# A fused two-block network: the SSM chunk-end products, their evictions and the scan, one projection tile later

## The chip, the cores and the metric

One core of a Trainium2 chip runs the whole program in one launch. The metric is device time in microseconds (us), as the median of several executions; lower is better. TensorE (PE, with PEld for its weight loads), VectorE (DVE), ScalarE (ACT), GpSimd (POOL) and SyncE (SP, which issues the weight loads) each run their own instruction stream in order and meet at semaphores.

## The reference, cut to what matters

The reference is two blocks one behind the other on 512 tokens of width 1024. The first is an attention and MLP network. The second is a hybrid layer: one projection gives queries, keys and values of 12 attention heads, the input `u` of a state space model (SSM) and two gates. The change sits in the second block, in the part that works on `u`:

```python
z = n @ w_in                       # 4 tiles of u, 12 heads x (q, k, v), gates
uf = u.astype(jnp.float32).reshape(B, S, SSM_GROUPS, SSM_GROUP)
bu_re = jnp.einsum('bsgc,gpc->bsgp', uf, bb_re)
bu_im = jnp.einsum('bsgc,gpc->bsgp', uf, bb_im)
_, _, h_re, h_im = lax.associative_scan(_complex_affine_combine, (ar, ai, bu_re, bu_im), axis=1)
y = (jnp.einsum('bsgp,gcp->bsgc', h_re, c_re.astype(jnp.float32))
     - jnp.einsum('bsgp,gcp->bsgc', h_im, c_im.astype(jnp.float32))
     + d_skip.astype(jnp.float32) * uf)
```

## The kernel before, in words

Every projection runs through one pipeline. A unit is a weight tile of 8x128x128 floats. SyncE loads it into `raw` (4 slots), ScalarE rounds it to `w_hi` (L1731, 2 slots), GpSimd computes the remainder `w_lo = raw - w_hi` (L919), and TensorE does 24 products of 128x512 for it (L1097, L1098, L1099, three for each of 8 slices). ScalarE makes the `w_hi` of tile t+1 when it comes to tile t, after tile t-1 has been finished on TensorE, and then does its own duties for tile t-1.

The second block's projection is one long list of tiles, `middle`: 4 tiles of `u`, then for each head n the tiles (n, 0) query, (n, 1) key and (n, 2) value, then the gates. The work of attention and of the SSM is hung on these tiles by hand, in each engine's `middle_after` or `middle_tile`. Behind tile (n, x) there come:

- TensorE, x = 0: the products of probabilities and values of head n-2 (L1556, L1555), the turning of the values of head n-1 (L1157) and its scores (`group_scores`, L1529). The scores wait for the semaphore `roped` of head n-1 and for `s_stored`. x = 2: the turning of the probabilities of head n-1 (L1157).
- VectorE, every tile: the eviction of the accumulator (L3211 and L3213, for values L3213 alone), after which the accumulator is free (`stored`). x = 0: masks and row maxima of head n-1 (`group_tops`, L3243, L3249). x = 2: `add_rotated` (L3224), which ends in `roped`, and at the end of the tile the eviction L3257 of the outputs of head n-1 (`group_outputs`).
- ScalarE, x = 0: the exponentials of head n-1. They wait for the negated maxima (L3249), and ScalarE's next `w_hi` stands behind them. x = 1: the two DMAs of `rotate`, which wait for the key tile's eviction. x = 2: copies of the turned probabilities.

The SSM works on chunks of 8 tokens. Its input goes out to DRAM and comes back by chunk as `u_chunk`: ScalarE issues four of the eight DMAs at tile (0, 0) and four at (0, 1). `chunk_ends` on TensorE (L1469) is 128 products of 64x64 into four PSUM banks, `keep_ends` on VectorE copies these banks to `state` (L3274), and `scan` on VectorE is a generator of 78 instructions: 35 large ones (L3141 to L3149, seven rounds of five, 128x256 or 128x128), 35 small ones (the same lines at 128x32 and 128x16) and 8 of 128x784 (L3166 to L3172, twice four). A table in VectorE's `middle_tile` says how many of them are issued behind each tile of heads 1 to 4. They come before `group_outputs` of an x = 2 tile, and behind the eviction of every tile. The end of the scan is waited for by TensorE at `ssm_outputs`, behind tile (5, 1).

The order on each engine is therefore the order of the code; no scheduler is in it. The lines that follow are those of the profile.

Of the kernel before, what the change touches and what calls it, by code (L numbers as in the profile page):

```python
# [207 lines left out]
def transposed_blocks_program(nc, a, out):  # L208
# [84 lines left out]
    with ctx:  # L293
# [383 lines left out]
        for i in range(8):  # L677
            for t in range(4):
# [3 lines left out]
                n = (hi - lo) * P  # L682
# [44 lines left out]
        def others(T, kind=""):  # L727

            b = take(T, kind)
            T.saw(f"{kind}full{b}")  # L730
            T.saw(f"{kind}stored{b}")
            return b
# [222 lines left out]
        def _(pe):  # L955
            T = start(pe)
# [619 lines left out]
            def middle_after(t):  # L1576
                kind, n, x = MID[t]
                if kind == "qkv":
                    if x == 0 and n:
                        if n > 1:  # L1580
                            group_values(n - 2)
                        turn_values(n - 1)
                        group_scores(n - 1)
                    if x == 2 and n:
                        turn_probs(n - 1)
                    if (n, x) == (1, 0):
                        chunk_ends()
                    if n == 5 and x:
                        ssm_outputs(x - 1)
                    if n in (9, 10) and x == 1:  # L1590
                        turn_outputs(n - 9)
                if kind == "gate_ssm":
                    if n == 0:
                        group_values(LAST_STEP - 1)
                        turn_values(LAST_STEP)
                        group_scores(LAST_STEP)
                    if n == 1:
                        group_values(LAST_STEP)
                        turn_rows()
                if (kind, n) in SPREAD_AT:  # L1600
                    spread_weights(SPREAD_AT[kind, n])
                if kind == "glu_b":
                    if n == 0:
                        turn_probs(LAST_STEP)
                if (kind, n) == ("gate_attn", 1):
                    T.saw("attended")
                    pe.wait_ge(sems["attended"], T.at("attended"))
# [97 lines left out]
        def _(act):  # L1705
            T = start(act)
# [578 lines left out]
            def middle_tile(m, s, t, b):  # L2285
                kind, n, x = MID[t]
                if kind == "u":
                    send_u(n, b)
                    if n == 3:
                        turn_angles()  # L2290
                if kind == "qkv":
                    if n == x == 0:
                        fetch_u(0, 4)
                    if x == 0:
                        if n > 1:
                            others(T, "o_")
                        if n:
                            copy_values(n - 1)
                            group_exponentials(n - 1)
                        if n == 1:  # L2300
                            for _ in range(2):
                                others(T, "t_")
                                others(T, "o_")
                    if x == 1:
                        rotate(n)
                        if n == 0:
                            fetch_u(4, CHUNK)
                    if x == 2:
                        T.saw("roped")
                        if n:  # L2310
                            copy_probs(n - 1)
                    if (n, x) == (2, 0):
                        fetch_toe()
                    if (n, x) == (3, 1):
                        fetch_ca()
                    if n == 5 and x:
                        keep_outputs(x - 1)
                    if n == 6 and x:
                        square_outputs(x - 1)
                    if n in (7, 8) and x == 2:  # L2320
                        gelu_gate(n - 7)
                    if n in (9, 10) and x == 1:
                        round_y(n - 9)
                G = gtmp[:, n % 2]
                if (kind, n) == ("gate_attn", 0):
                    round_attention(3)
                if kind in ("gate_ssm", "gate_attn"):
                    stored(b)
                    fn(G[:, 0, :], G[:, 0, :], ACT.Sigmoid).then_inc(sems["gate"], T.up("gate"))
                if kind == "gate_ssm":  # L2330
                    if n == 0:
                        others(T, "o_")
                        copy_values(LAST_STEP)
                        group_exponentials(LAST_STEP)
                    if n == 1:
                        others(T, "o_")
                    if n == 1:
                        for _ in range(2):
                            others(T, "t_")
                    if n == 4:  # L2340
                        round_shares()
                for _ in SPREAD_AT.get((kind, n), ()):
                    others(T, "o_")
                if kind == "glu_a":
                    if n in (6, 7):
                        round_attention(n - 5)
                if kind == "glu_b":
                    act.wait_ge(sems[f"full{b}"], T.at(f"full{b}"))
                    if n >= 2:
                        act.wait_ge(sems["gated"], T.at("gated", 1))  # L2350
                    fn(G[:, 1, :], acc2[b], ACT.Sigmoid).then_inc(sems[f"stored{b}"], T.up(f"stored{b}"))
                    T.saw("gated")
                    if n == 2:
                        weigh()
                    if n == 5:
                        round_attention(0)
                    if n == 0:
                        copy_probs(LAST_STEP)
                if kind == "attn":
                    T.saw("gated")  # L2360
                    act.wait_ge(sems["gated"], T.at("gated"))
                    fn(mixed_hi[:, n, :], G[:, 0, :], ACT.Copy).then_inc(sems["mixed_hi"], T.up("mixed_hi"))
# [90 lines left out]
        def _(dve):  # L2453
# [813 lines left out]
            def keep_ends():  # L3267

                v.memset(state[:, :, :, 0:1], 0.0).then_inc(sems["dve"], T.up("dve"))
                for ri, kind in ((0, "t_"), (1, "o_")):  # L3270
                    for f in range(2):
                        b = result(T, kind)
                        dve.wait_ge(sems[f"{kind}full{b}"], T.at(f"{kind}full{b}"))
                        v.tensor_copy(state[:, ri, 8 * f:8 * f + 8, 1:],  # L3274
                                      (tps, ops_)[ri][b].rearrange("p (j k) -> p j k", j=8)).then_inc(
                            sems[f"{kind}stored{b}"], T.up(f"{kind}stored{b}"))
                for kind in ("t_stored0", "t_stored1", "o_stored0", "o_stored1"):
                    dve.wait_ge(sems[kind], T.at(kind))
# [115 lines left out]
            def middle_tile(m, s, t, b):  # L3394
# [9 lines left out]
                if kind == "qkv":  # L3404
                    if (n, x) == (0, 0):
                        make_tables()
                    group_tile(n, x, b)
                    if x == 2:
                        add_rotated(n)
                    if x == 0 and n:  # L3410
                        others(T, "t_")
                        group_tops(n - 1)
                        if n == 1:
                            keep_ends()
                    if x == 2 and n:
                        probs_turned(n - 1)
                    if (n, x) == (0, 1):
                        invert_root_h()
                    if 1 <= n <= 4 and (n, x) != (1, 0):
                        for _ in range(((0, 8, 8), (4, 7, 7), (9, 10, 10), (7, 4, 4))[n - 1][x]):  # L3420
                            next(scanning, None)
                    if n == 5:
                        if x == 0:
                            assert not list(scanning)
                        else:
                            for _ in range(2):
                                others(T, "o_")
                    if n and x == 2:
                        group_outputs(n - 1)
                    if n in (7, 8) and x == 1:  # L3430
                        cube(n - 7)
                    if n in (8, 9) and x == 2:
                        gate_y(n - 8)
                    if n in (9, 10) and x == 1:
                        rest_of_y(n - 9)
# [179 lines left out]
```

## Time and profile before

| what | value |
|---|---|
| median of 3 runs | 2124.36 us (2124.08 to 2124.7) |
| the profiled execution's own time | 2126.04 us |
| its span | 2124.2 us |
| TensorE busy | 2109.9 us (99%) |
| TensorE weight loads busy | 1804.1 us (85%) |
| VectorE busy | 1127.6 us (53%) |
| GpSimd busy | 873.1 us (41%) |
| ScalarE busy | 818.2 us (39%) |
| granted TensorE clock, mean | 0.998 of full |

The shares are means over the whole span. The stretch in question, tile (1, 0) to tile (5, 1), runs from about 1237 to 1340 us. In a timeline each row has start, duration, engine, line, operation, out<-in, how many; what stands in brackets is the idle time before it and what ended it. An instruction that is queued behind a running one or blocked in its access shows as a long duration and not as idle time.

### The profile page before, as it was taken

What the parts mean: (1) busy time and instruction counts of PE and PEld (TensorE: products, weight loads), DVE (VectorE), ACT (ScalarE), POOL (GpSimd) and SP (SyncE); (2) the same over time, 40 slices, a digit from 0 to 9 for tenths busy, and PEclk for the clock granted to TensorE, in tenths of its full rate; (3) what the DMA queues carried; (4) which work ended last, traced back from release to release, by engine and by line L of the source; (5) the groups of instructions that cost most, each with busy time, mean ns of one, the idle gap of its engine ahead of it and who ended that gap; (6) DMA issues with size and microseconds to landing.
All of it is one profiled execution on the core that took longest, in us unless ns stands there. A gap on an engine that the chain in (4) does not pass through costs nothing.

```text
span 2124.2 us, 33781 instructions
## 1 busy us (share of the span) xinstructions
PE 2109.9 (99%) x13386; PEld 1804.1 (85%) x13386; DVE 1127.6 (53%) x1701; ACT 818.2 (39%) x1362; POOL 873.1 (41%) x379
## 2 busy tenths in 40 slices
PE   9999999999999999999999999999999999999998
PEld 9987899999999777888888788888887788888887
DVE  6678766525632476420333579566774644543125
ACT  5258544223323584421333323344433432322224
POOL 3313434434444554444444433243444444444442
PEclk9999999999999999999999999999999999999999
DMA  6610245343434403333333465233233233333331
GB/s 178 168 56 2 56 140 144 90 120 103 137 90 134 133 2 92 97 95 94 92 96 94 134 130 153 79 86 86 86 88 95 87 112 89 99 89 92 89 101 66
DMA packets 375411, 210.77 MB, mean 99 GB/s; under 512 B 26659, under 2 KB 367876, under 8 KB 374392
## 3 DMA queue, kind: packets, MB, share of 16 engines
q1 hardware_dynamic: 364974, 192.61, 31.8%
q10 hardware_dynamic: 10314, 16.41, 2.8%
q8 instruction: 90, 1.47, 0.3%
q14 instruction: 33, 0.27, 0.0%
HBM read 196.97 MB, written 15.40 MB: 100 GB/s over the span
## 4 chain that ended last, share of the span: by engine, by line
PE 59%; issue 27%; POOL 12%; DVE 0%; ACT 0%; DMA 0%; POOLq 0%; SPq 0%; DVEq 0%; ACTq 0%
PE acc L1097 15%; PE acc L1098 15%; PE acc L1099 15%; POOL w_lo L919 12%; PE acc L1185 3%; PE ops L1254 2%; PE tps L1194 1%; PE acc L979 1%; PE ops L1248 1%; PE acc L980 1%; PE acc L981 1%; PE tps L1157 1%; DMA xin<-in_x 0%; PE ops L1409 0%; SPq L740 0%
## 5 line engine op out<-in xcount | busy, mean ns | idle before, releaser
L919 POOL TENSOR_TENSOR w_lo<-raw,w_hi 128x1024 fp32r<-128x1024 f32 x326 | 800.1, 2454 | 1126.5 <-ACT w_hi L1731 1116.0
L1731 ACT ACTIVATE w_hi<-raw 128x1024 fp32r<-128x1024 f32 x325 | 344.5, 1060 | 1005.5 <-PE acc L1099 985.7
L1097 PE MATMUL acc<-hr_hi,w_hi 128*128 128x512 f32 x1056 | 421.4, 399 | 0.1
L1099 PE MATMUL acc<-hr_hi,w_lo 128*128 128x512 f32 x1056 | 417.7, 396 | 0.0
L1098 PE MATMUL acc<-hr_lo,w_hi 128*128 128x512 f32 x1056 | 417.6, 395 | 0.0
L1097 PE MATMUL acc<-hn_hi,w_hi 128*128 128x264 f32 (+1 forms) x840 | 246.7, 294 | 0.0
L1099 PE MATMUL acc<-hn_hi,w_lo 128*128 128x264 f32 (+1 forms) x840 | 244.2, 291 | 0.0
L1098 PE MATMUL acc<-hn_lo,w_hi 128*128 128x264 f32 (+1 forms) x840 | 244.2, 291 | 0.0
L1097 PEld LDWEIGHTS acc<-hr_hi,w_hi 128*128 128x128 f32 x1056 | 198.5, 188 | 48.6 <-issue 1.1
L1099 PEld LDWEIGHTS acc<-hr_hi,w_lo 128*128 128x128 f32 x1056 | 198.4, 188 | 47.9
L1098 PEld LDWEIGHTS acc<-hr_lo,w_hi 128*128 128x128 f32 x1056 | 198.5, 188 | 47.3 <-issue 0.7
L1098 PEld LDWEIGHTS acc<-hn_lo,w_hi 128*128 128x128 f32 x840 | 158.3, 188 | 2.7
L1097 PEld LDWEIGHTS acc<-hn_hi,w_hi 128*128 128x128 f32 x840 | 158.2, 188 | 2.8
L1099 PEld LDWEIGHTS acc<-hn_hi,w_lo 128*128 128x128 f32 x840 | 157.5, 188 | 2.5
L1097 PE MATMUL acc<-mid_hi,w_hi 128*128 128x264 f32 x512 | 145.5, 284 | 0.0
L1098 PE MATMUL acc<-mid_lo,w_hi 128*128 128x264 f32 x512 | 145.0, 283 | 0.0
L1099 PE MATMUL acc<-mid_hi,w_lo 128*128 128x264 f32 x512 | 145.0, 283 | 0.0
L942 POOL TENSOR_SCALAR probs<-probs,stat 128x528 f32<-128x528 f32 (+2 forms) x49 | 72.8, 1486 | 104.5 <-DVE stat L2581 104.5
L1097 PE MATMUL acc<-mr_hi,w_hi 128*128 128x512 f32 x256 | 101.2, 396 | 0.0
L1098 PE MATMUL acc<-mr_lo,w_hi 128*128 128x512 f32 x256 | 101.2, 396 | 0.0
L1099 PE MATMUL acc<-mr_hi,w_lo 128*128 128x512 f32 x256 | 101.2, 396 | 0.0
L1097 PEld LDWEIGHTS acc<-mid_hi,w_hi 128*128 128x128 f32 x512 | 96.4, 188 | 0.2 <-issue 0.2
(486 smaller groups left out, 3755.6 us busy)
## 6 DMA issues: line engine op xcount, KB each, us to landing
raw<-in_w_up SPq DMA_DIRECT2D x64, 512.0 KB, 4.0
raw<-in_w_down SPq DMA_DIRECT2D x64, 512.0 KB, 3.9
raw<-in_w_in SPq DMA_DIRECT2D x56, 512.0 KB, 3.8
raw<-in_w_ffn_gate SPq DMA_DIRECT2D x22, 512.0 KB, 3.7
raw<-in_w_ffn_up SPq DMA_DIRECT2D x22, 512.0 KB, 3.8
raw<-in_w_in_even SPq DMA_DIRECT2D x18, 512.0 KB, 7.1
raw<-in_w_ffn_down SPq DMA_DIRECT2D x16, 512.0 KB, 3.8
raw<-in_w_in_odd SPq DMA_DIRECT2D x10, 512.0 KB, 5.4
```

The source lines that it names most:

```text
L919: nc.gpsimd.tensor_tensor(w_lo[:, part], raw[:, slot], w_hi[:, part].bitcast(F32), ALU.subtract).then_inc(sems["lo"], T.up("lo"))
L942: nc.gpsimd.tensor_scalar(S, S, st[:, 4:5], None, ALU.mult).then_inc(sems["scaled"], T.up("scaled"))
L979: mm(out, w_hi[:, part, k, :], x_hi, start=first, stop=False)
L980: mm(out, w_hi[:, part, k, :], x_lo, start=False, stop=False)
L981: return mm(out, w_lo[:, part, k, :], x_hi, start=False, stop=last)
L1097: mm(out, w_hi[:, part, w0 + k, :], xh, start=s0, stop=False)
L1098: mm(out, w_hi[:, part, w0 + k, :], xl, start=False, stop=False)
L1099: ins = mm(out, w_lo[:, part, w0 + k, :], xh, start=False, stop=s1)
L1157: ins = nc.tensor.transpose(out(t), x, ident[k:k + x.shape[0], k:k + x.shape[0]])
L1185: ins = mm(bank[rows, c:c + w], q, keys, start=first, stop=last)
L1254: ins = mm(ops_[b][rows, to], p.v[o][k], weights(o, k)[:, queries], start=k == 0, stop=k == last)
L1731: fn(w_hi[:, n % 2], raw[:, n % 4], ACT.Copy).then_inc(sems["hi"], T.up("hi"))
```

## The change

The chunk-end products, their evictions and the bookkeeping of their banks on ScalarE move from tile (1, 0) to tile (1, 1). The scan starts behind tile (1, 2) instead of (1, 1). Its table goes from 0, 8, 8 / 4, 7, 7 / 9, 10, 10 / 7, 4, 4 for the tiles of heads 1, 2, 3, 4 to 0, 0, 9 / 6, 9, 9 / 9, 10, 10 / 9, 7, 4. The new numbers sum to 82, so the generator runs out at tile (4, 1), one tile earlier than before.

```diff
@@ TensorE, middle_after
-                    if (n, x) == (1, 0):
+                    if (n, x) == (1, 1):
                         chunk_ends()
@@ ScalarE, middle_tile
-                        if n == 1:
-                            for _ in range(2):
-                                others(T, "t_")
-                                others(T, "o_")
+                    if (n, x) == (1, 1):
+                        for _ in range(2):
+                            others(T, "t_")
+                            others(T, "o_")
@@ VectorE, middle_tile
-                        if n == 1:
-                            keep_ends()
+                    if (n, x) == (1, 1):
+                        keep_ends()
...
-                    if 1 <= n <= 4 and (n, x) != (1, 0):
-                        for _ in range(((0, 8, 8), (4, 7, 7), (9, 10, 10), (7, 4, 4))[n - 1][x]):
+                    if 1 <= n <= 4 and (n, x) > (1, 1):
+                        for _ in range(((0, 0, 9), (6, 9, 9), (9, 10, 10), (9, 7, 4))[n - 1][x]):
                             next(scanning, None)
```

On TensorE, behind tile (1, 0), the order before is as follows. L1157 and L1529 are the turned values and the scores of head 0, L1469 the chunk ends, L1097 to L1099 a projection tile.

```order
L1157 MATMUL tps<-ident,qkv 128x128 x4
L1529 MATMUL acc<-qkv 128x128
L1529 MATMUL acc<-qkv 128x256 x3
L1469 MATMUL tps<-u_chunk,ends_w 64x64 x32
L1469 MATMUL ops<-u_chunk,ends_w 64x64 x32
L1097 MATMUL acc<-hr_hi,w_hi 128x512
```

In the changed kernel the same products stand behind tile (1, 1), whose last products are the first rows here.

```order
L1098 MATMUL acc<-hr_lo,w_hi 128x512
L1099 MATMUL acc<-hr_hi,w_lo 128x512
L1469 MATMUL tps<-u_chunk,ends_w 64x64 x32
L1469 MATMUL ops<-u_chunk,ends_w 64x64 x32
L1097 MATMUL acc<-hr_hi,w_hi 128x512
```

So a whole tile of 24 products now lies between the scores of head 0 and the chunk ends. On VectorE, in the key tile (2, 1) and up to the rotation L3224 in the value tile (2, 2), there stands before:

```order
L3213 TENSOR_TENSOR qkv<-acc,rope_c 128x512
L3141 TENSOR_TENSOR scan_tmp<-state,a_pow 128x256
L3143 TENSOR_TENSOR scan_tmp<-state,a_pow 128x256
L3145 TENSOR_TENSOR state<-state,scan_tmp 128x32x8
L3147 TENSOR_TENSOR state<-state,scan_tmp 128x16x8
L3149 TENSOR_TENSOR state<-state,scan_tmp 128x16x8
L3141 TENSOR_TENSOR scan_tmp<-state,a_pow 128x256
L3143 TENSOR_TENSOR scan_tmp<-state,a_pow 128x256
L3213 TENSOR_TENSOR qkv<-acc,rstd 128x512
L3224 TENSOR_TENSOR qkv<-qkv,rot_s 32x1024
```

and in the changed kernel:

```order
L3213 TENSOR_TENSOR qkv<-acc,rope_c 128x512
L3141 TENSOR_TENSOR scan_tmp<-state,a_pow 128x256
L3143 TENSOR_TENSOR scan_tmp<-state,a_pow 128x256
L3145 TENSOR_TENSOR state<-state,scan_tmp 128x32x8
L3147 TENSOR_TENSOR state<-state,scan_tmp 128x16x8
L3149 TENSOR_TENSOR state<-state,scan_tmp 128x16x8
L3141 TENSOR_TENSOR scan_tmp<-state,a_pow 128x256
L3143 TENSOR_TENSOR scan_tmp<-state,a_pow 128x256
L3145 TENSOR_TENSOR state<-state,scan_tmp 128x32x8
L3147 TENSOR_TENSOR state<-state,scan_tmp 128x16x8
L3213 TENSOR_TENSOR qkv<-acc,rstd 128x512
L3224 TENSOR_TENSOR qkv<-qkv,rot_s 32x1024
```

Two scan instructions more stand ahead of the rotation of head 2 in this tile. On VectorE again, from the key tile (4, 1) to the rotation of head 4, before:

```order
L3213 TENSOR_TENSOR qkv<-acc,rope_c 128x128x4
L3166 TENSOR_TENSOR scan_tmp<-state,a_pow 128x784
L3168 TENSOR_TENSOR scan_tmp<-state,a_pow 128x784
L3170 TENSOR_TENSOR state<-state,scan_tmp 128x16x7x7
L3172 TENSOR_TENSOR state<-state,scan_tmp 128x16x7x7
L3213 TENSOR_TENSOR qkv<-acc,rstd 128x128x4
L3224 TENSOR_TENSOR qkv<-qkv,rot_s 32x1024
```

and in the changed kernel:

```order
L3213 TENSOR_TENSOR qkv<-acc,rope_c 128x128x4
L3168 TENSOR_TENSOR scan_tmp<-state,a_pow 128x784
L3170 TENSOR_TENSOR state<-state,scan_tmp 128x16x7x7
L3172 TENSOR_TENSOR state<-state,scan_tmp 128x16x7x7
L3166 TENSOR_TENSOR scan_tmp<-state,a_pow 128x784
L3168 TENSOR_TENSOR scan_tmp<-state,a_pow 128x784
L3170 TENSOR_TENSOR state<-state,scan_tmp 128x16x7x7
L3172 TENSOR_TENSOR state<-state,scan_tmp 128x16x7x7
L3213 TENSOR_TENSOR qkv<-acc,rstd 128x128x4
L3224 TENSOR_TENSOR qkv<-qkv,rot_s 32x1024
```

All four instructions that stood behind the rotation of head 4 are now ahead of it, and one of the eight has moved to tile (4, 0).

## Rows read from the trace of the kernel before

**Rows 1.** The page: the span, and busy time by engine.

```profile
span 2124.2 us, 33781 instructions
PE 2109.9 (99%) x13386; PEld 1804.1 (85%) x13386; DVE 1127.6 (53%) x1701; ACT 818.2 (39%) x1362; POOL 873.1 (41%) x379
```

**Rows 2.** TensorE's waits over the whole span: us in total, times, longest.

```profile
PE tps L1469 <- DMA u_chunk<-u_d: 1.6, 1, 1.6
...
PE acc L1097 <- POOL w_lo L919: 0.2, 1, 0.2
```

**Rows 3.** Timeline of TensorE behind tile (1, 0): start, us, instruction.

```profile
1242.93 1.68 PE L1529 MATMUL acc<-qkv 128*128 128x128 f32 x8
1246.26 2.08 PE L1469 MATMUL tps<-u_chunk,ends_w 128*64 128x64 f32 x64 [1.65 <-DMA u_chunk<-u_d]
...
1250.14 0.50 PE L1097 MATMUL acc<-hr_hi,w_hi 128*128 128x512 f32 x1
```

**Rows 4.** Timeline of TensorE behind tile (2, 0).

```profile
1269.79 1.68 PE L1529 MATMUL acc<-qkv 128*128 128x128 f32 x8
1271.12 0.58 PE L1097 MATMUL acc<-hr_hi,w_hi 128*128 128x512 f32 x1
```

**Rows 5.** Timeline of TensorE: behind (1, 2); head 2's scores; tile (3, 2); head 4's scores.

```profile
1261.44 0.93 PE L1157 MATMUL tps<-ident,probs 128*128 128x128 f32 x7
...
1290.86 1.68 PE L1529 MATMUL acc<-qkv 128*128 128x128 f32 x8
...
1297.97 0.40 PE L1097 MATMUL acc<-hr_hi,w_hi 128*128 128x512 f32 x1
...
1333.07 1.06 PE L1529 MATMUL acc<-qkv 128*128 128x128 f32 x8
```

**Rows 6.** Timeline of VectorE: a round of the scan and tile (3, 0)'s eviction.

```profile
1292.88 0.44 DVE L3149 TENSOR_TENSOR state<-state,scan_tmp 128x128 f32<-128x128 f32 x1
...
1295.69 0.68 DVE L3257 COPY o<-ops 128x512 f32<-128x512 f32 x1
...
1296.88 0.67 DVE L3213 TENSOR_TENSOR qkv<-acc,rope_c 128x512 f32<-128x512 f32 x1
```

**Rows 7.** Timeline of VectorE from the end of tile (1, 1)'s eviction to head 2's rotation.

```profile
1257.35 0.64 DVE L3141 TENSOR_TENSOR scan_tmp<-state,a_pow 128x256 f32<-128x256 f32 x1
...
1263.32 2.71 DVE L3145 TENSOR_TENSOR state<-state,scan_tmp 128x256 f32<-128x256 f32 x1
...
1288.08 0.69 DVE L3213 TENSOR_TENSOR qkv<-acc,rstd 128x512 f32<-128x512 f32 x1
1288.87 1.21 DVE L3224 TENSOR_TENSOR qkv<-qkv,rot_s 32x1024 f32<-32x1024 f32 x1
1290.01 0.62 DVE L3145 TENSOR_TENSOR state<-state,scan_tmp 128x256 f32<-128x256 f32 x1
```

**Rows 8.** Timeline of GpSimd: the remainders made after tiles (3, 0), (3, 2) and (5, 0).

```profile
1290.25 2.53 POOL L919 TENSOR_TENSOR w_lo<-raw,w_hi 128x1024 fp32r<-128x1024 f32 x1 [3.75 <-ACT w_hi L1731]
...
1306.17 2.40 POOL L919 TENSOR_TENSOR w_lo<-raw,w_hi 128x1024 fp32r<-128x1024 f32 x1 [2.44 <-ACT w_hi L1731]
...
1332.47 2.36 POOL L919 TENSOR_TENSOR w_lo<-raw,w_hi 128x1024 fp32r<-128x1024 f32 x1 [4.03 <-ACT w_hi L1731]
```

**Rows 9.** Timeline of VectorE: head 3's rotation, then tiles (4, 1) and (4, 2).

```profile
1306.31 3.34 DVE L3224 TENSOR_TENSOR qkv<-qkv,rot_s 32x1024 f32<-32x1024 f32 x1
...
1319.31 1.10 DVE L3211 TENSOR_TENSOR rot_t<-acc,rope_s 32x512 f32<-32x512 f32 x1 [2.26 <-PE acc L1099]
...
1322.07 0.94 DVE L3168 TENSOR_TENSOR scan_tmp<-state,a_pow 128x784 f32<-128x784 f32 x1
1323.04 3.06 DVE L3170 TENSOR_TENSOR state<-state,scan_tmp 128x784 f32<-128x784 f32 x1
...
1329.31 1.09 DVE L3213 TENSOR_TENSOR qkv<-acc,rstd 128x512 f32<-128x512 f32 x1
1330.48 1.21 DVE L3224 TENSOR_TENSOR qkv<-qkv,rot_s 32x1024 f32<-32x1024 f32 x1
```

## The prediction

> **What bounds the kernel now.** I read the page first, for the span and the engines. TensorE is busy for 2109.9 of 2124.2 us, no other engine for more than 53% [rows 1]. So the end moves only where TensorE waits, or waits anew. The list of TensorE's waits is short: the longest one in the part of the program that is changed is 1.6 us for the DMA that brings `u_chunk`, and the only other one there is 0.2 us for a `w_lo` [rows 2]. Then I read the timeline of TensorE behind tile (1, 0), where the wait is, and after that VectorE's timeline up to tile (5, 0), because the change takes scan work out of two tiles and puts it into others. There the reader is to see that VectorE is busy without a gap from tile (1, 1) to tile (4, 0) and runs behind TensorE all that time, although its share of the whole span is only half. The question is what in this stretch still comes in time.
>
> **Part 1, the wait that goes.** The scores of head 0 start at 1242.93 and the chunk ends at 1246.26 [rows 3]. Behind tile (2, 0) the same eight score products are followed by the next product after 1.33 us (1269.79 to 1271.12) [rows 4]. So without the wait TensorE would go on at 1244.26, and the wait costs 2.0 us (1.65 by the idle time in brackets; I take the start times). In the changed kernel tile (1, 1) starts at 1244.26, and the chunk ends come one tile, 5.65 us, later, at about 1249.9. The data were there at 1246.26, so 3.7 us are in hand. The products themselves take the same 3.9 us (1246.26 to 1250.14) [rows 3] wherever they stand. Gain: 2.0 us. ScalarE's edit is bookkeeping and issues nothing; no DMA moves. The four copies of `keep_ends` fall between the evictions of (1, 1) and (1, 2), where VectorE now has nothing else: no cost. The 0.2 us wait for a `w_lo` [rows 2] stands before tile (5, 0), where the product of 0.94 us that opens the last scan part has left the place beside that `w_lo`; I credit 0.1 us.
>
> From here on I keep the clock of the old trace and shift the new kernel by those 2.0 us, so that TensorE's places are the old ones as long as it doesn't wait.
>
> **Part 2, VectorE up to head 2.** A round of five large scan instructions takes 2.81 us (1292.88 to 1295.69) [rows 6], 0.56 us each. One instruction in each `w_lo` takes far longer: L3145 took 2.71 us at 1263.32 and 0.62 at 1290.01 [rows 7], and L3224 3.34 us at 1306.31, just behind the start of a `w_lo` at 1306.17 (2.40 us) [rows 8, 9], against 1.21 [rows 7]. While GpSimd works on a `w_lo`, a VectorE instruction with both inputs in SBUF stands still, 2.1 us each time; L3211 and L3213, which read PSUM, do not.
>
> The Trainium skill says the same ("SBUF — State Buffer", the section with the two physically separate sides): a VectorE instruction with two SBUF inputs and a GpSimd instruction that reads SBUF exclude each other for the whole instruction. By that rule the cost of a moved scan step hangs on what it stands beside, and these rows agree.
>
> Before, VectorE needed 30.7 us from the end of (1, 1)'s eviction (1257.35) to the eviction L3213 of the value tile (2, 2) (1288.08) [rows 7], with 27 scan instructions and five such blocks (2.0, 2.1, 2.1, 1.0, 2.1 us). Now it can't start before tile (1, 2) is there: the row 1261.44 [rows 5] follows that tile's last product, which ends at 1261.6. It has 24 instructions in this stretch, 1.7 us less, and four blocks. I take all four at 2.1, since the one that cost 1.0 fell mostly on an eviction; together 0.9 us less. 1261.65 + 30.7 - 1.7 - 0.9 = 1289.8, so it comes 1.7 us later than before, measured against TensorE.
>
> **Part 3, the new wait at head 2 or 3.** The rotation L3224 stands 0.8 us behind that eviction, so it would start at 1290.6. Before it started at 1288.87 and ended at 1290.08, and the scores of head 2, which wait for it, started at 1290.86 [rows 5, 7]: 0.8 us in hand. Now a `w_lo` starts at 1290.25 [rows 8], before it. Blocked like the one of head 3, it ends 1.08 us behind the end of the `w_lo`: 1290.25 + 2.36 + 1.08 = 1293.7, and TensorE waits 2.8 us. What is queued on TensorE behind the scores is the whole tile (3, 1). The first slip, of 0.35 us between 1290.25 and 1290.6, is small, so take the other case: the rotation is just in front, ends by 1291.4, and the wait is 0.5 us. Then the block falls on the scan behind it, as before, and that tile has 9 instructions against 7: the eviction of (3, 0), which ended at 1297.55 [rows 6], ends 1.7 + 1.1 = 2.8 us later, at 1300.3, while tile (3, 2), which uses that accumulator, started at 1297.97 [rows 5]. With the 0.5 us this gives a second wait of 1.9 us, 2.4 in all. The two cases answer alike. Bounds: 0, if VectorE is over 2 us faster than I count, and 4.9, if one more block falls in. I take 2.8.
>
> **Part 4, heads 3 and 4.** The wait of part 3 gives VectorE its lag back. In tile (3, 2) and tile (4, 0) two scan instructions more each are issued, most of them small, about 1.6 us in all with the one of 128x784 (0.97 us from 1322.07 to 1323.04 [rows 9]). Before (4, 1) VectorE was idle for 2.26 us [rows 9], which covers this. Tile (4, 1) is different. Before, it had four instructions of 128x784 and the other four stood behind the rotation of head 4; now all of the remaining seven stand ahead of it. Three more at 0.97 are 2.9 us, and L3213 of tile (4, 2) goes from 1329.31 to 1332.2, the rotation from 1330.48 [rows 9] to 1333.4. A `w_lo` starts at 1332.47 [rows 8], so this rotation is blocked too: 1332.47 + 2.36 + 1.08 = 1335.9. The scores of head 4 started at 1333.07 [rows 5]. Wait: 2.8 us. Not blocked it would be 1.5 us (1330.48 + 1.21 + 2.9 = 1334.6); the row at 1332.47 is a full 0.9 us ahead, so I take 2.8. Lower bound 0, since 1.4 us were in hand before and an unused 1 us in tile (4, 1) could give back the rest; upper bound 4.9 with another block.
>
> The end of the scan was waited for by nobody and comes earlier now. Behind (5, 0) both kernels are alike, and TensorE has no other wait that could swallow a difference.
>
> **Sum.** -2.0 - 0.1 + 2.8 + 2.8 = +3.5 us on the profiled span of 2124.2, thus 2127.7. That execution's own time was 2126.04, 1.7 above the median, so I apply the difference to the median of the runs: 2124.36 + 3.5 = 2127.9 us, 0.16% slower. About 0.2%, 4.2 us, is what a measurement of this kernel can tell from no change.
>
> **Rivals.** (a) Only the removed wait counts: VectorE keeps up everywhere, -2.1 us, 2122.3. For it: the two rotations had 0.8 and 1.4 us in hand, and the scores of head 1 get several us of room. Against it: VectorE starts its unbroken stretch 4.3 us later (1257.35 to 1261.65) and has only 1.7 + 0.9 us less to do. (b) The waits come but without the blocks: the rotations late by 1.0 us (1290.6 + 1.21 against 1290.86) and 1.5 us; -2.1 + 1.0 + 1.5 = +0.4, 2124.8. For it: the first margin is 0.35 us. Against it: by part 3 what doesn't hit the rotation hits an eviction. A mix of (b) with the forecast, one wait full and the other small, lies at +1 to +2. (c) On the other side of the 0.2%: a further block of 2.1 us in front of a rotation, as VectorE, drifting by tenths against GpSimd, meets two `w_lo` between two evictions where I count one. From one such meeting on the sum is +5.6, 2130.0. For it: one rotation took the long form already before [rows 9]. Against it: `w_lo` comes only once in a tile. (d) The change doesn't remove the wait, because the data come later: +0 in part 1, then 2129.9. The 3.7 us in hand speak against it.
>
> **Chances.** Forecast (2126.6 to 2129) 0.46; (b) and the mix 0.24; (a) 0.15; (c) 0.13; (d) 0.02. Over 2128.6 lie (c), (d) and the upper edge of the forecast, 0.05: slower 0.20. Faster by over 0.2% would mean under 2120.1; the removed wait can't give it: 0.02. The rest, 0.78, is within. The range takes in (a) at 2122.3 and most of the forecast's upper side: 2122.0 to 2129.8. Without (a) the likeliest case has 2126.6 to 2129.
>
> **What would show it.** Right: the chunk ends follow tile (1, 1) with no idle time; TensorE shows a wait for L3224 at the scores of head 2 (or for L3213 at tile (3, 2)) of 2 to 3 us, and one for L3224 at the scores of head 4; both L3224 take over 3 us beside a `w_lo`. Wrong: L3224 of head 2 ends before TensorE's place, or the blocks fall on evictions that read PSUM and cost nothing; then (a) or (b). A wait anywhere behind tile (5, 1) that was not there before would be something I haven't seen.

## The result and the profile after

| | median, us | runs | span, us |
|---|---|---|---|
| before | 2124.36 | 7 (2123.31 to 2124.79) | 2124.2 (own time 2126.04) |
| after | 2131.39 | 7 (2131.01 to 2132.42) | 2129.5 (own time 2131.25) |

The ratio is 1.0034, with a 95% interval of 1.0022 to 1.0046: the changed kernel is 7.0 us slower. The forecast was +3.5 us, and 2131.39 lies outside the predicted range, which ended at 2129.8. The prediction was wrong.

The page of the changed kernel, against [rows 1]:

```profile
span 2129.5 us, 33778 instructions
PE 2111.9 (99%) x13386; PEld 1805.6 (85%) x13386; DVE 1123.9 (53%) x1701; ACT 818.1 (38%) x1362; POOL 872.5 (41%) x379
```

The shares are the same to a per cent. Nothing on this page says what happened. It is in TensorE's waits over the whole span (us in total, times, longest), against [rows 2]:

```profile
PE acc L1529 <- DVE qkv L3224: 4.7, 2, 2.7
PE ops L1674 <- DVE sq L3576: 2.1, 1, 2.1
...
PE tps L1157 <- DVE qkv L3213: 0.5, 1, 0.5
```

The wait of L1469 for `u_chunk` is gone. Two waits of the scores L1529 for the rotation and one of the turned values for an eviction are new; that of L1674 is far behind the change and in both kernels. TensorE's timeline of the changed kernel has them at the places of [rows 3] (head 0's scores, then the chunk ends one tile later) and [rows 5] (heads 2 and 4):

```profile
1242.85 1.68 PE L1529 MATMUL acc<-qkv 128*128 128x128 f32 x8
1244.18 0.58 PE L1097 MATMUL acc<-hr_hi,w_hi 128*128 128x512 f32 x1
...
1250.07 2.08 PE L1469 MATMUL tps<-u_chunk,ends_w 128*64 128x64 f32 x64
...
1259.65 0.93 PE L1157 MATMUL tps<-ident,probs 128*128 128x128 f32 x7
...
1291.95 1.79 PE L1529 MATMUL acc<-qkv 128*128 128x128 f32 x8 [2.71 <-DVE qkv L3224]
1293.38 0.58 PE L1097 MATMUL acc<-hr_hi,w_hi 128*128 128x512 f32 x1
...
1334.38 0.66 PE L1157 MATMUL tps<-ident,qkv 128*128 128x128 f32 x4 [0.47 <-DVE qkv L3213]
1337.07 1.16 PE L1529 MATMUL acc<-qkv 128*128 128x128 f32 x8 [2.03 <-DVE qkv L3224]
1337.98 0.48 PE L1097 MATMUL acc<-hr_hi,w_hi 128*128 128x512 f32 x1
...
1340.37 0.63 PE L1097 MATMUL acc<-hr_hi,w_hi 128*128 128x512 f32 x1
1340.80 0.63 PE L1098 MATMUL acc<-hr_lo,w_hi 128*128 128x512 f32 x1
...
1342.17 0.39 PE L1099 MATMUL acc<-hr_hi,w_lo 128*128 128x512 f32 x1
1342.41 0.39 PE L1097 MATMUL acc<-hr_hi,w_hi 128*128 128x512 f32 x1
...
1345.29 0.66 PE L1487 MATMUL ops<-toe_in,u_chunk 128*64 128x128 f32 x8
```

Look at the products behind the last wait. Those at 1340.37 and 1340.80 start 0.43 us apart, those at 1342.17 and 1342.41 0.24 us. The windows of the same trace (us, PE busy, granted clock, DMA share, GB/s) say why:

```profile
1334.00:1337.00 3.00, 0.66 (x4) 1.00 0.00 0
1337.00:1339.00 2.00, 1.94 (x11) 0.84 0.89 255
1339.00:1341.00 2.00, 2.00 (x6) 0.50 0.02 7
1341.00:1343.00 2.00, 2.00 (x9) 0.81 0.00 0
```

TensorE was busy for 0.66 of 3 us, while it waited. Once it works again, the granted clock is 0.50, which is 1.2 instead of 2.4 GHz, for part of tile (5, 1). PE is fully busy in these rows; this loss is no idle time and no view of waits shows it.

The other side of the two waits is on VectorE. Its timeline in the changed kernel, against [rows 7, 9]:

```profile
1287.83 0.67 DVE L3213 TENSOR_TENSOR qkv<-acc,rstd 128x512 f32<-128x512 f32 x1
1288.59 3.30 DVE L3224 TENSOR_TENSOR qkv<-qkv,rot_s 32x1024 f32<-32x1024 f32 x1
...
1333.28 1.05 DVE L3213 TENSOR_TENSOR qkv<-acc,rstd 128x512 f32<-128x512 f32 x1
1334.42 2.59 DVE L3224 TENSOR_TENSOR qkv<-qkv,rot_s 32x1024 f32<-32x1024 f32 x1
```

and GpSimd's, against [rows 8]:

```profile
1288.47 2.34 POOL L919 TENSOR_TENSOR w_lo<-raw,w_hi 128x1024 fp32r<-128x1024 f32 x1 [2.68 <-ACT w_hi L1731]
...
1333.58 2.35 POOL L919 TENSOR_TENSOR w_lo<-raw,w_hi 128x1024 fp32r<-128x1024 f32 x1 [3.96 <-ACT w_hi L1731]
```

Both rotations, 1.21 us in [rows 7, 9], start behind a `w_lo` and end 1.1 us behind its end (1290.81 to 1291.89, 1335.93 to 1337.01). The `w_lo` was 0.12 us ahead at head 2 and 0.84 us at head 4.

### The profile page after: what moved, and what is told of

It reads as the page before. It is cut to its first block, busy times and chain, and to the rows that moved or that the text cites. A ratio compares the mean times of both kernels' runs of the same rounds, so it can differ in the third digit from the quotient of the medians.

```text
span 2129.5 us, 33778 instructions
## 1 busy us (share of the span) xinstructions
PE 2111.9 (99%) x13386; PEld 1805.6 (85%) x13386; DVE 1123.9 (53%) x1701; ACT 818.1 (38%) x1362; POOL 872.5 (41%) x379
## 4 chain that ended last, share of the span: by engine, by line
PE 59%; issue 28%; POOL 12%; DVE 0%; ACT 0%; POOLq 0%; DVEq 0%; ACTq 0%
PE acc L1097 15%; PE acc L1098 15%; PE acc L1099 15%; POOL w_lo L919 12%; PE acc L1185 3%; PE ops L1254 2%; PE tps L1194 1%; PE acc L979 1%; PE ops L1248 1%; PE acc L981 1%; PE acc L980 1%; PE tps L1157 1%; PE acc L1283 0%; PE ops L1409 0%; PE tps L979 0%
## 5 line engine op out<-in xcount | busy, mean ns | idle before, releaser
L1097 PE MATMUL acc<-hr_hi,w_hi 128*128 128x512 f32 x1056 | 422.2, 400 | 0.1
L1099 PE MATMUL acc<-hr_hi,w_lo 128*128 128x512 f32 x1056 | 418.4, 396 | 0.0
L1097 PE MATMUL acc<-hn_hi,w_hi 128*128 128x264 f32 (+1 forms) x840 | 246.8, 294 | 0.0
L1099 PE MATMUL acc<-hn_hi,w_lo 128*128 128x264 f32 (+1 forms) x840 | 244.2, 291 | 0.0
L1097 PEld LDWEIGHTS acc<-hr_hi,w_hi 128*128 128x128 f32 x1056 | 198.9, 188 | 48.6 <-issue 1.1
L1099 PEld LDWEIGHTS acc<-hr_hi,w_lo 128*128 128x128 f32 x1056 | 198.8, 188 | 47.9
L1097 PEld LDWEIGHTS acc<-hn_hi,w_hi 128*128 128x128 f32 x840 | 158.2, 188 | 2.8
L1099 PEld LDWEIGHTS acc<-hn_hi,w_lo 128*128 128x128 f32 x840 | 157.5, 188 | 2.4
L1097 PE MATMUL acc<-mid_hi,w_hi 128*128 128x264 f32 x512 | 145.5, 284 | 0.0
L1099 PE MATMUL acc<-mid_hi,w_lo 128*128 128x264 f32 x512 | 145.0, 283 | 0.0
L1097 PE MATMUL acc<-mr_hi,w_hi 128*128 128x512 f32 x256 | 101.2, 396 | 0.0
L1099 PE MATMUL acc<-mr_hi,w_lo 128*128 128x512 f32 x256 | 101.2, 396 | 0.0
L1097 PEld LDWEIGHTS acc<-mid_hi,w_hi 128*128 128x128 f32 x512 | 96.4, 188 | 0.2 <-issue 0.2
```

The lines of the kernel that those rows point to most:

```text
L1097: mm(out, w_hi[:, part, w0 + k, :], xh, start=s0, stop=False)
L1099: ins = mm(out, w_lo[:, part, w0 + k, :], xh, start=False, stop=s1)
```

## The experiments

Where nothing else is said, the edit is one line of the changed kernel, VectorE's table of scan instructions per tile, and the diff shows that line alone. "Half clock" says whether windows between 1225 and 1350 us have a granted clock of about 0.5. Waits are those of the one profiled execution. Ratios are against the kernel before on the same chip.

| run | median, us (runs) | ratio, 95% interval | new TensorE waits 1225 to 1350, us | half clock |
|---|---|---|---|---|
| before_again | 2124.14 (10) | 0.9997, 0.9988 to 1.0007 | none | no |
| move_light | 2124.88 (11) | 1.0003, 0.9994 to 1.0012 | 0.4 | no |
| move_even | 2124.21 (11) | 0.9999, 0.9990 to 1.0008 | 0.3 | no |
| first_only | 2127.70 (11) | 1.0013, 1.0004 to 1.0023 | 2.7 | no |
| second_only | 2132.16 (6) | 1.0035, 1.0022 to 1.0047 | 3.9, 1.0, 0.5 | yes |
| dose_76 | 2129.13 (11) | 1.0020, 1.0011 to 1.0029 | 0.9, 0.4, 2.1 | yes |
| two_less | 2131.75 (5) | 1.0035, 1.0022 to 1.0049 | 2.7, 0.5, 2.0 | twice |
| table_only | 2131.69 (6) | 1.0032, 1.0019 to 1.0044 | 2.7, 2.0, 0.5; `u_chunk` 0.5 | twice |
| late_u_before | 2124.93 (11) | 1.0003, 0.9994 to 1.0012 | `u_chunk` 1.0 | no |
| late_u_light | 2124.64 (11) | 1.0003, 0.9994 to 1.0012 | 0.9, at tile (4, 0) | no |
| kept_busy | 2130.26 (7) | 1.0028, 1.0017 to 1.0040 | 0.45, 0.46, 0.45 | no |
| after_again | 2132.87 (5) | 1.0038, 1.0024 to 1.0052 | 2.7, 2.05, 0.46 | yes, elsewhere |

**before_again**: the kernel before, unchanged.

> The kernel before, unchanged, profiled once more. Its first profiled execution had a span of 2124.2 us and an own time of 2126.04, 1.7 above its median of 2124.36, while the changed kernel's profiled execution (2131.25) lies at its median. Theory 1: the wait for u_chunk at the chunk ends (2.0 us by start times in the first profile) varies with the landing of the DMA and is usually some 0.3 us; then this profile shows an own time near 2124.4, a span near 2122.6 and a wait under 0.6 us. Rival: the wait is always 1.6 to 2.0 us and the 1.7 us came from elsewhere, for instance a spell of lower clock at the end; then the row of the wait reads 1.6 again at a span of 2122.6.

Its span was 2122.4 us, its own time 2124.19. TensorE's timeline behind tile (1, 0) shows no wait at the chunk ends:

```profile
1242.74 1.68 PE L1529 MATMUL acc<-qkv 128*128 128x128 f32 x8
1244.36 2.09 PE L1469 MATMUL tps<-u_chunk,ends_w 128*64 128x64 f32 x64
...
1248.24 0.50 PE L1097 MATMUL acc<-hr_hi,w_hi 128*128 128x512 f32 x1
```

L1469 comes 1.62 us behind L1529, against 3.33 in [rows 3]. The eight DMAs of `u_chunk` landed sooner, after 4.5 us in the median and at most 8.0, against 5.8 and 10.3 in the trace of [rows 3] (both from the views of DMA issues). So the wait differs between executions of one kernel. In table_only below, where the chunk ends stand in the old place too, it is 0.55 us. From here on the trace of before_again is the one to compare with.

**move_light**, **move_even**: the move, with the scan's weight kept away from heads 2 and 4.

```diff
-((0, 0, 9), (6, 9, 9), (9, 10, 10), (9, 7, 4))
+((0, 0, 9), (4, 7, 7), (9, 10, 10), (9, 9, 4))    # move_light
+((0, 0, 9), (4, 7, 7), (6, 13, 10), (9, 9, 4))    # move_even
```

> The changed kernel with the products, their evictions and the scan's start one tile later as in the change, but the scan's table 0,0,9 / 4,7,7 / 9,10,10 / 9,9,4: 20 instead of 24 scan instructions ahead of head 2's rotation, 74 instead of 78 ahead of head 4's. Theory (the loss is the lateness of the two rotations alone): neither L3224 wait nor the spell of half clock appears, and the time is 2122.4 to 2124.1, that is the kernel before less its wait for u_chunk (2.0 us or, if that is usually shorter, 0.3 us). Rival (moving the products costs something itself, at the banks or at the copies): 2126 or more with a wait at L1469, L3274 or tile (1, 2).

> The moved chunk ends with the table 0,0,9 / 4,7,7 / 6,13,10 / 9,9,4: three scan instructions of tile (3, 0) go behind (3, 1), because the kernel with 9, 10, 10 there (2124.88 us) still showed a wait of 0.4 us at tile (4, 0) for the eviction of (3, 1). Theory: that wait goes and no other comes, 2124.0 to 2124.4 us, which is the kernel before at its usual landing of u_chunk (2124.4) less at most 0.3: no measurable gain from the move. Rival (there is a gain of the size of the first profile's wait, 1.7 to 2 us): 2122.7 or less. If VectorE's lag turns up elsewhere, 2125 or more.

Both medians are within 0.5 us of the kernel before on the same chip, where the interval of a ratio is 2 us wide to either side. The time expected of move_light, 2122.4 to 2124.1, was missed by 0.8 us: no gain showed. In each, TensorE has one small wait, at tile (4, 0), which move_even was meant to take away and only made smaller. Its row in move_even:

```profile
1302.82 0.50 PE L1097 MATMUL acc<-hr_hi,w_hi 128*128 128x512 f32 x1 [0.26 <-DVE qkv L3213]
```

So the move is free if the scan's weight is placed well, and it brings nothing that these runs can show.

**first_only**: head 2's load as in the change, tile (4, 1) with 3 instructions instead of 7.

```diff
-((0, 0, 9), (6, 9, 9), (9, 10, 10), (9, 7, 4))
+((0, 0, 9), (6, 9, 9), (9, 10, 10), (9, 3, 4))
```

> The changed kernel with the last row of the table 9,3,4 instead of 9,7,4, so that four of the eight 128x784 instructions stand behind head 4's rotation again. Theory: the wait of 2.7 us at head 2's scores stays, the waits of 0.5 and 2.0 us at tile (5, 0) and the 3.4 us of half clock behind them go; the time falls by 4.0 us (0.5 + 2.0 + 1.5), to 2127.4. Rival (the clock falls because of the first wait and only shows late): a spell of half clock remains and the time is 2128.9 or more.

The wait of 2.7 us is there alone, and the scores of head 4 come 91.33 us behind those of head 0 (1243.41 to 1334.74) against 88.46 in before_again: 2.87 us, part 3 of the prediction by itself. The clock stays whole behind this wait:

```profile
1293.00:1300.00 7.00, 7.00 (x32) 1.00 0.23 68
```

**second_only**, **dose_76**: head 2 light, head 4 heavy, in two doses.

```diff
-((0, 0, 9), (6, 9, 9), (9, 10, 10), (9, 7, 4))
+((0, 0, 9), (4, 7, 7), (9, 10, 10), (11, 11, 0))    # second_only
+((0, 0, 9), (4, 7, 7), (9, 10, 10), (9, 11, 2))     # dose_76
```

> The changed kernel with the table 0,0,9 / 4,7,7 / 9,10,10 / 11,11,0: no wait at head 2, but all 78 scan instructions ahead of head 4's rotation as in the change. Theory: no wait at head 2's scores; the waits at tile (5, 0) are there, rather longer than 2.5 us in all, since the first wait no longer gives VectorE time and one more 128x784 instruction stands in (4, 1): 2.5 to 4.5 us, with the spell of half clock. Time 2127.5 to 2129.5. Rival (VectorE's lag is only there because of the first wait): no wait, 2124.

> The changed kernel with the table 0,0,9 / 4,7,7 / 9,10,10 / 9,11,2: 76 scan instructions ahead of head 4's rotation, where the kernel of 74 (table ending 9,9,4) had no wait at tile (5, 0) and 2124.9 us, and the one of 78 (ending 11,11,0) waits of 3.9 and 0.5 us, a spell of half clock and 2132.2 us. Theory (each 128x784 instruction more is 0.97 us, and a block of 2.1 us comes in once the rotation starts after the w_lo): waits of 1 to 3 us at tile (5, 0). If the clock falls only behind the longer waits, as behind 2.5 and 4.4 us and not behind 2.7 us at head 2, this one decides whether 2 us at this place are enough: without the spell 2126.5 to 2127.5, with it 2128 to 2129. Rival (all or nothing by the block): 2.1 us or more, as with 78.

In second_only the waits at tile (5, 0) are 4.3 us, as expected (2.5 to 4.5), and one of 1.0 us at tile (4, 0) was not foreseen. The time, 2132.16, missed the expected 2127.5 to 2129.5. TensorE's timeline:

```profile
1335.82 0.83 PE L1157 MATMUL tps<-ident,qkv 128*128 128x128 f32 x4 [3.85 <-DVE qkv L3213]
1337.12 2.07 PE L1529 MATMUL acc<-qkv 128*128 128x128 f32 x8 [0.47 <-DVE qkv L3224]
```

and VectorE's, from tile (4, 1) on:

```profile
1325.85 3.05 DVE L3172 TENSOR_TENSOR state<-state,scan_tmp 128x784 f32<-128x784 f32 x1
...
1331.83 3.00 DVE L3172 TENSOR_TENSOR state<-state,scan_tmp 128x784 f32<-128x784 f32 x1
1334.75 1.02 DVE L3213 TENSOR_TENSOR qkv<-acc,rstd 128x512 f32<-128x512 f32 x1
1335.86 1.21 DVE L3224 TENSOR_TENSOR qkv<-qkv,rot_s 32x1024 f32<-32x1024 f32 x1
```

Here the `w_lo` catches a scan instruction ahead of the eviction (3.00 us instead of 0.97), and the rotation is whole at 1.21 us. The block is the same, what stands in it is not, and the rotation ends where it ended in after (1337.07 against 1337.01 us). The wait is longer because TensorE gets there 1.9 us sooner (1331.97 against 1333.91), with 1.0 us of waiting behind it instead of 2.7. In dose_76 the waits at tile (5, 0) are 2.5 us (again with 0.9 us at tile (4, 0) besides) and the half clock comes too, in the window behind the scores of head 4:

```profile
1337.00:1340.00 3.00, 3.00 (x11) 0.66 0.01 2
```

**two_less**: two scan instructions fewer ahead of head 2's rotation, two more behind it.

```diff
-((0, 0, 9), (6, 9, 9), (9, 10, 10), (9, 7, 4))
+((0, 0, 9), (6, 7, 11), (9, 10, 10), (9, 7, 4))
```

> The changed kernel with 7 instead of 9 scan instructions behind tile (2, 1) and 11 instead of 9 behind (2, 2); all else as in the change. Head 2's rotation then starts some 0.7 us earlier, at 1287.8 on the changed kernel's clock, before the w_lo of 1288.47, and is not blocked. Theory 1 (the prediction's part 3, both cases answer alike): no wait at head 2's scores, but the blocked instruction is now one of the scan ahead of the eviction of (3, 0), which ends near 1299, while tile (3, 2) is due at 1296.4: a wait of about 2.6 us for L3213 at tile (3, 2), and the time stays within 0.7 us of the changed kernel's 2131.4. Rival (the 2.7 us hang on the blocked rotation alone): no wait of over 1 us before tile (4, 0), 2128.7.

VectorE's timeline: the rotation is whole, the block falls on the next scan instruction, and the eviction of (3, 0) is late.

```profile
1287.09 1.21 DVE L3224 TENSOR_TENSOR qkv<-qkv,rot_s 32x1024 f32<-32x1024 f32 x1
1288.24 2.82 DVE L3145 TENSOR_TENSOR state<-state,scan_tmp 128x256 f32<-128x256 f32 x1
...
1297.77 0.67 DVE L3213 TENSOR_TENSOR qkv<-acc,rope_c 128x512 f32<-128x512 f32 x1
```

TensorE waits for that eviction at tile (3, 2):

```profile
1298.50 0.80 PE L1097 MATMUL acc<-hr_hi,w_hi 128*128 128x512 f32 x1 [2.67 <-DVE qkv L3213]
```

The prediction's "the two cases answer alike" holds: 2.71 us at one place, 2.67 at the other. This time the clock fell behind the first wait as well (0.50 in the window 1298 to 1301).

**table_only**: the kernel before, its chunk ends where they were, with the scan's new start and table alone.

```diff
-if 1 <= n <= 4 and (n, x) != (1, 0):
-    for _ in range(((0, 8, 8), (4, 7, 7), (9, 10, 10), (7, 4, 4))[n - 1][x]):
+if 1 <= n <= 4 and (n, x) > (1, 1):
+    for _ in range(((0, 0, 9), (6, 9, 9), (9, 10, 10), (9, 7, 4))[n - 1][x]):
```

> The kernel before with nothing moved but the scan: chunk ends and their copies stay behind tile (1, 0), the scan starts behind (1, 2) and has the change's table 0,0,9 / 6,9,9 / 9,10,10 / 9,7,4. Theory: all of the loss is the table's, so the waits of 2.7 us at head 2's scores and of 0.5 and 2.0 us at tile (5, 0) and the spell of half clock are as in the changed kernel, and the time is 2131.4 plus 0.3 us, within 1 us. Rival (the products at their new place cost something): at least 1.5 us below the changed kernel.

The median is within 0.3 us of the changed kernel's, and TensorE has the same three waits (the profiled execution was the slowest of its runs, 5 us above their median, so only its waits and the clock behind them are read). The loss is in the table; where the chunk ends stand costs nothing that these runs can show. The half clock is there behind both waits.

**late_u_before**, **late_u_light**: four of the DMAs that bring `u_chunk` issued one tile later, in the kernel before and in move_light.

```diff
                     if x == 1:
                         rotate(n)
+                    if x == 2:
                         if n == 0:
                             fetch_u(4, CHUNK)
-                    if x == 2:
                         T.saw("roped")
```

> The kernel before with the second four DMAs of u_chunk issued by ScalarE at tile (0, 2) instead of (0, 1), 5.6 us later. Theory (the wait at the chunk ends is the landing of the last u_chunk against TensorE's place, and in most executions the landing is just in time): TensorE waits 5 to 7.5 us at L1469 and the time is 2129.5 to 2132, perhaps 1.5 us more by a spell of half clock. Rival (there is room of some us in the usual execution): less than 3 us.

> The same later issue of u_chunk in the kernel with the chunk ends one tile later and the table 0,0,9 / 4,7,7 / 9,10,10 / 9,9,4 (2124.88 us as it stands). Theory: the move gives 5.65 us of room, so the wait is the former kernel's less 5.65, 0 to 2 us, and the time 2124.9 to 2127. Rival (the products would wait for something else at their new place): 2128 or more.

The first missed: a wait of 1.0 us, not 5 to 7.5. The last of the eight DMAs was issued only 3.4 us later, not 5.6 (at 1239.3 us against 1235.9 in before, where the four stand behind the two DMAs of `rotate`), and the transfers then landed in at most 6.9 us. Within what it gave, the theory holds: the same lateness makes TensorE wait for `u_chunk` in the kernel before (1.0 us) and not with the move, whose one wait is that of move_light at tile (4, 0). The move does buy room at the chunk ends, but room that is seldom needed.

**kept_busy**, **after_again**: in the first, dummy products (10 ahead of head 2's scores, 7 ahead of head 4's) fill the time in which TensorE would wait for the rotation. They go to the place in PSUM that the scores then overwrite. The second is the changed kernel unchanged, for the same chip.

```diff
-                pe.wait_ge(sems["roped"], T.at("roped"))
                 pe.wait_ge(sems["s_stored"], T.at("s_stored"))
+                for x in range({2: 10, 4: 7}.get(n, 0)):
+                    mm(acc[x % 2][:, 1, 0:512], hr_hi[:, 0, 0:P], hr_hi[:, 0, 0:512], start=True, stop=True)
+                pe.wait_ge(sems["roped"], T.at("roped"))
```

> The changed kernel, with ten products of 128x512 in front of head 2's scores and seven in front of head 4's, written into the scores' own place in PSUM and overwritten by them: 2.3 and 1.6 us of work that nobody needs, inside the waits for L3224 of 2.7 and 2.0 us. The waits' ends are set by VectorE and stay where they were. Theory (the half clock of 3.4 us behind tile (5, 0), 1.5 us of time, comes from TensorE standing still): no spell, 2129.9 us. Rival (the spell has nothing to do with the standing still): a spell as before and 2131.4. Were the waits not what sets the time, the products would add up to 3.9 us: 2135.

> The changed kernel unchanged, beside the one above and on the same chip: 2131.4 us, its waits at L3224 of 2.7 and 2.0 us and a spell of half clock behind the second again.

TensorE in kept_busy, in place of the long waits (the edit shifts the later line numbers by 2: L1531 are the scores, L3226 is the rotation):

```profile
1289.80 2.56 PE L1526 MATMUL acc<-hr_hi 128*128 128x512 f32 x10
1292.81 1.79 PE L1531 MATMUL acc<-qkv 128*128 128x128 f32 x8 [0.45 <-DVE qkv L3226]
...
1335.64 1.86 PE L1526 MATMUL acc<-hr_hi 128*128 128x512 f32 x7
1337.95 1.16 PE L1531 MATMUL acc<-qkv 128*128 128x128 f32 x8 [0.45 <-DVE qkv L3226]
```

Its windows behind head 4's scores:

```profile
1337.00:1340.00 3.00, 2.55 (x16) 1.00 0.58 172
1340.00:1343.00 3.00, 3.00 (x15) 1.00 0.01 3
```

Counted from head 0's scores (1243.66 here, 1242.85 in after), the scores come where they came in the changed kernel: after 49.15 and 94.29 us, against 49.10 and 94.22. What comes sooner is L1487 behind tile (5, 1), after 100.97 us (1344.63) against 102.44. In the median the kernel is 2.6 us faster than after_again. Its seven runs lie within 1.1 us, with a mean granted clock of 0.998 or 0.999 in each; the five of after_again lie within 2.9 us, and the clock is 0.997 in four of them. And in after_again the half clock is at another place. TensorE's timeline and windows at head 2:

```profile
1291.80 3.36 PE L1529 MATMUL acc<-qkv 128*128 128x128 f32 x8 [2.71 <-DVE qkv L3224]
1294.60 0.99 PE L1097 MATMUL acc<-hr_hi,w_hi 128*128 128x512 f32 x1
...
1307.52 0.93 PE L1157 MATMUL tps<-ident,probs 128*128 128x128 f32 x7
```

```profile
1292.00:1295.00 3.00, 3.00 (x9) 0.50 0.56 166
1295.00:1298.00 3.00, 3.00 (x9) 0.51 0.01 3
...
1340.00:1343.00 3.00, 3.00 (x18) 1.00 0.57 168
```

From these scores to the turning L1157 it takes 15.72 us, against 12.81 in after (1291.95 to 1304.76) and in kept_busy: 2.9 us for this half clock. The same wait of 2.71 us brought no half clock in after and first_only; behind head 4's wait it is the other way round (whole here, half in after).

The Trainium skill ("TensorE: Matmul & The Clock Gate", Part 1) says that the chip's watch over TensorE's activity runs free, not tied to the start of a kernel, and that the number of slow products therefore differs between runs of one kernel. The two traces agree, with the half clock at about 1338 to 1342 us in after and at 1292 to 1298 in after_again. No run here shows where that watch stood.

## Why the prediction was wrong

TensorE's marks in the two traces, from their timelines:

| start of | before_again | after | behind by | added |
|---|---|---|---|---|
| head 0's scores | 1242.74 | 1242.85 | 0.11 | |
| turning behind tile (1, 2) | 1259.55 | 1259.65 | 0.10 | 0.0 |
| head 2's scores | 1288.97 | 1291.95 | 2.98 | 2.9 |
| tile (3, 1) | 1290.30 | 1293.38 | 3.08 | 0.1 |
| turned values of head 4 | 1330.76 | 1334.38 | 3.62 | 0.5 |
| head 4's scores | 1331.20 | 1337.07 | 5.87 | 2.3 |
| tile (5, 1) | 1332.01 | 1337.98 | 5.97 | 0.1 |
| L1487 behind tile (5, 1) | 1337.79 | 1345.29 | 7.50 | 1.5 |

That is 7.4 us added between the first and the last mark, against 7.1 by the spans and 7.0 by the medians. What the marks have too much is at the end of the program, where TensorE waits 2.1 us for L3576 in both kernels. These are the products behind that wait in before_again and in after:

```profile
2115.42 1.01 PE L1674 MATMUL ops<-ones,sq 128*128 128x1 f32 x4 [2.09 <-DVE sq L3576]
...
2122.90 0.61 PE L1674 MATMUL ops<-ones,sq 128*128 128x1 f32 x4 [2.08 <-DVE sq L3576]
```

Here after is still 7.48 us behind, and at the next instruction 7.07 (2116.30 to 2123.37). The granted clock is 0.50 from 2115 to 2117 us in before_again, and 0.80 from 2122.5 to 2124 in after. So in this pair of traces the kernel before paid 0.4 us of half clock there.

**Part 1 failed, in its size.** "Gain: 2.0 us" was 1.7 us even in that one trace: from L1529 to the turning behind (1, 2) it took 18.51 us in [rows 3, 5], and 16.80 in after. The 1.33 us that the prediction took from behind tile (2, 0) is too short for this place; before_again needs 1.62 us from L1529 to L1469 without a wait. And before_again takes 16.81 over the same stretch, so against it the removed wait is worth 0.0 us. The sign was on the table: the profiled execution's own time was 1.7 us above the median, and the wait cost 1.7 us. The prediction named the 1.7 us and then took a difference from that execution, with the wait in it, off the median of other runs. Of the three executions profiled with the chunk ends and their DMAs in the old place, one has the full wait, one 0.55 us (table_only) and one none. With 0.0 here, the same working would have given +5.5, 2129.9, which is the number of rival (d). That table_only is as slow as the changed kernel, though it doesn't move the chunk ends, fits this.

**The 0.1 us for the `w_lo` before tile (5, 0)** is 0.0, and [rows 2] was misread. The wait of 0.2 us is not in the changed part: it stands at 1643.46 us in before, in front of a product of `mixed_hi`, and is the same in before_again and after.

**Part 2 held.** It put the eviction of (2, 2) at 1289.8 in the old clock, 1287.8 with the 2.0 us taken off; it ended up at 1287.83.

**Part 3 held**, 2.71 us of idle time and 2.9 by the marks against 2.8. The rotation was to end at 1291.7 and ended at 1291.89. The other branch of its argument, if the `w_lo` had come a little later, was run in two_less and gave 2.67.

**Part 4 held in its mechanism**: eviction forecast at 1333.0, measured 1333.28, and the rotation blocked. The wait is split: 0.47 us for the eviction and 2.03 for the rotation, 2.5 in all, 2.8 by the marks. The sign "both L3224 take over 3 us" came only at head 2; at head 4 it is 2.59 us, and the prediction's own working (1333.4 to 1335.9) had 2.5. Rivals (a) and (b), which had VectorE in time or unblocked, are ruled out for this table, and (c) as well, since no further block came. (d) is ruled out as a mechanism: no data came late, and the wait at L1469 is gone, but it was not a fixed cost before.

**What the prediction lacked is a term behind its waits.** It ended each wait where TensorE resumes, at the full clock. Behind head 4's wait 24 products took 7.31 us (1337.98 to 1345.29) instead of 5.78 (1332.01 to 1337.79), 1.5 us more. kept_busy supports the cause: with TensorE active in place of most of the idle time the half clock was gone in its profile and the kernel faster, though its scores come no sooner. Its edit also orders the two semaphores differently, so the median alone is not the proof; the clock rows and the 1.5 us between the marks are.

So the miss of 3.5 us (7.0 against 3.5) is, by the marks, 2.1 for two gains that did not exist (2.0 and 0.1), 1.5 of half clock, 0.2 for restarting behind two waits and 0.1 in the waits themselves (5.7 against 5.6), 3.9 in all, less the 0.4 at the program's end. The two gains alone would have moved the forecast from 2127.9 to 2130.0, out of its range; the half clock alone, to 2129.4, would not. What is left open is why one execution loses the clock behind head 2 and one behind head 4. first_only's eleven times run from 2126.4 to 2128.7, and the mean granted clock of the runs goes with them, 0.999 in the three fastest and 0.997 in the three slowest. A clock lower by 0.002 over 2125 us is 4.3 us at half clock, which costs 2.1 us (an estimate from these rounded figures). So a stretch of half clock behind its one long wait in the slower runs would explain the spread, but the only one profiled, at 2127.70, had none there.

## What to carry to other kernels

Before a wait is priced from one profile, compare that execution's own time with the median of the runs: a distance the size of the wait suggests that the wait is not usually there, and a second profile can tell. A table that deals one engine's filler work between another's tiles should be judged by what stands just ahead of the instructions that are waited for, and by where the other engine's blocking instruction falls; shifting two fillers moved the wait by a tile without changing it. And a wait of 2 to 3 us on a TensorE that is otherwise busy can have a price beyond its idle time, here 1.5 us in one execution and 2.9 in another, so look at the granted clock there.

## What the runs showed of the hardware

- Between 1285 and 1345 us, where TensorE is otherwise busy, the traces have eleven waits of 2.5 to 4.3 us, those at head 4 in two parts. Eight were followed by a granted clock of 0.50 and three were not (head 2 in after and first_only, head 4 in after_again). Behind waits of up to 1.0 us, and behind the 1.65 us in before, it stayed at 1.00. It cost 1.5 us in after and 2.9 in after_again. With 17 dummy products in place of most of the idle time it was gone.
- A VectorE instruction with both inputs in SBUF that starts 0.12 us behind a `w_lo` stands through all of it (3.30 us instead of 1.21), and one that starts 0.85 us ahead of it is whole (1.21 us, two_less), with the block passed to the next. The prediction had that.
- `u_chunk`'s transfers landed in 5.8, 4.5 and 5.1 us in the median in three executions (before, before_again, after) that issue them alike, and in 10.3, 8.0 and 8.6 us at most. A wait that hangs on such a DMA differs from execution to execution.
